# The feed-forward input of a streaming encoder step: eight block products against seven

## What is computed

```python
    x = x + gt1 * (merged @ w_out)
    h2 = rmsnorm(x, g_norm[1]) * (1 + sc2) + sh2
    u, gg = jnp.split(h2 @ w_ffn_in, 2, axis=-1)
    x = x + gt2 * ((jax.nn.silu(gg) * u) @ w_ffn_out)
```

## Time and profile before

| | |
|---|---|
| median of 3 runs | 1094.04 us (1091.89 to 1094.91) |
| profiled execution | span 1095.1 us, and no time around the span is listed |
| TensorE busy | 1045.0 us, 95% of the span |
| VectorE, ScalarE, GpSimd busy | 395.5, 366.5, 368.7 us |
| mean granted clock of TensorE | 0.980 |
| loads of the feed-forward input | 44 of 512 KB, 4.6 us from issue to landing |
| wait at the start of the feed-forward output | 0.3 us of TensorE, for GpSimd's `w_lo` |

### The profile page before, as it was taken

One profiled execution on the slowest core, in us unless ns is written; L12 is line 12 of the kernel. 1 busy time (PEld: TensorE's weight loads), 2 busy tenths in 40 slices (PEclk: granted clock), 3 DMA queues, 4 the chain that ended last, 5 costly groups with the idle time before them and its releaser, 6 DMA issues.

```text
span 1095.1 us, 25416 instructions
## 1 busy us (share of the span) xinstructions
PE 1045.0 (95%) x10988; PEld 966.9 (88%) x10988; DVE 395.5 (36%) x926; ACT 366.5 (33%) x745; POOL 368.7 (34%) x252
## 2 busy tenths in 40 slices
PE   6999999999998988989898999999999999999997
PEld 3899989999996766777787999999999999999997
DVE  4400000194045676566556576222222222200003
ACT  4443333353444444345232233322322232211112
POOL 2165433343316061401160333333343334344331
PEclk8899999999999999899998999999999999999999
DMA  9986666343311000020341532233222322132322
GB/s 358 352 276 235 234 206 198 99 139 119 113 42 36 18 7 22 13 82 3 131 130 43 198 116 58 77 92 99 77 77 83 107 78 65 55 104 79 92 67 82
DMA packets 118174, 122.23 MB, mean 112 GB/s; under 512 B 5396, under 2 KB 102848, under 8 KB 115656
## 3 DMA queue, kind: packets, MB, share of 16 engines
q1 hardware_dynamic: 112864, 111.86, 31.8%
q10 hardware_dynamic: 5224, 9.10, 2.5%
HBM read 108.33 MB, written 15.23 MB: 113 GB/s over the span
## 4 chain that ended last, share of the span: by engine, by line
PE 86%; DVE 7%; issue 3%; ACT 3%; POOL 1%; ACTq 1%; DVEq 0%; POOLq 0%
PE ps L1566 83%; PE ps L1917 2%; DVE s_sb L1306 1%; PE ps L1817 1%; POOL w_lo L595 1%; DVE s_sb L1340 1%; ACT x_sq L743 0%; DVE xn L1118 0%; DVE gring L1477 0%; DVE Pb L1277 0%; DVE y_sb L1549 0%; DVE mt L1479 0%; ACT mgh L1031 0%; DVE XX L1287 0%; ACTq L729 0%
## 5 line engine op out<-in xcount | busy, mean ns | idle before, releaser
L595 POOL TENSOR_TENSOR w_lo<-w_raw,w_hi 128x2048 fp32r<-128x2048 f32 (+1 forms) x66 | 282.3, 4277 | 564.0 <-ACT w_hi L753 544.9
L1566 PE MATMUL ps<-hh,w_hi 128*128 128x274 f32 x1376 | 290.0, 293 | 2.7 <-DVE hl L1128 2.0
L1566 PE MATMUL ps<-hh,w_lo 128*128 128x274 f32 x1376 | 288.1, 292 | 0.0
L1566 PE MATMUL ps<-hl,w_hi 128*128 128x274 f32 x1376 | 286.6, 291 | 0.0
L1566 PEld LDWEIGHTS ps<-hh,w_hi 128*128 128x128 f32 x1376 | 219.0, 190 | 12.8 <-issue 11.2
L1566 PEld LDWEIGHTS ps<-hh,w_lo 128*128 128x128 f32 x1376 | 218.7, 190 | 0.8 <-issue 0.8
L1566 PEld LDWEIGHTS ps<-hl,w_hi 128*128 128x128 f32 x1376 | 219.0, 190 | 0.0
L753 ACT ACTIVATE w_hi<-w_raw 128x2048 fp32r<-128x2048 f32 (+1 forms) x66 | 117.5, 1781 | 106.6 <-PE ps L1566 101.1
L1566 PE MATMUL ps<-ah,w_hi 128*128 128x274 f32 x352 | 75.3, 290 | 0.3 <-POOL w_lo L595 0.3
L1566 PE MATMUL ps<-ah,w_lo 128*128 128x274 f32 x352 | 75.4, 290 | 0.0
L1566 PE MATMUL ps<-al,w_hi 128*128 128x274 f32 x352 | 75.2, 290 | 0.0
(11 more groups left out here) (375 smaller groups left out, 1537.8 us busy)
## 6 DMA issues: line engine op xcount, KB each, us to landing
w_raw<-in_w_ffn_in SPq DMA_DIRECT2D x44, 512.0 KB, 4.6
w_raw<-in_w_in SPq DMA_DIRECT2D x42, 512.0 KB, 5.0
ada_l<-in_w_ada SPq DMA_DIRECT2D x16, 1024.0 KB, 6.4
ada_w<-in_w_ada SPq DMA_DIRECT2D x8, 1024.0 KB, 13.6
w_raw<-in_w_ffn_out SPq DMA_DIRECT2D x16, 384.0 KB, 4.0
w_raw<-in_w_ffn_out SPq DMA_DIRECT2D x16, 320.0 KB, 3.4
g_d<-gst SPq DMA_DIRECT2D x16, 274.0 KB, 2.4
gring<-g_d SPq DMA_DIRECT2D x16, 274.0 KB, 3.2
```

The source lines that it names most:

```text
L595: pool.tensor_tensor(w_lo[:, s, 0:cols], w_raw[:, s, 0:cols], w_hi[:, s, 0:cols].bitcast(F32), ALU.subtract).then_inc(lo_done, 1)
L1566: return pe.matmul(out, lhsT, rhs, start=start, stop=stop)
```

## The change

From the second unit on, the feed-forward input is a product of 2 x 2 blocks in Winograd's form of Strassen's method. The blocks of the weight: gate and up columns, even and odd inner blocks. The blocks of the tokens: the two halves of 274, even and odd inner blocks. Seven products of 4 inner blocks each take the place of eight. The new parts:

- `token_sums`: four sums of token blocks for each pair of inner blocks, on VectorE into `tq`, in the output projection, behind every second tile. `token_high` rounds them on ScalarE (1096 columns), `token_low` subtracts on GpSimd.
- `raw_sums` and `second_sums`: four sums of weight blocks (512 columns) for each unit, on VectorE, written into PSUM banks 4 to 7.
- `block_high` rounds the seven weight blocks of 512 columns on ScalarE. `block_low` on VectorE takes the low part of the four summed ones, `blocks_low` on GpSimd that of the three plain ones. `ws_hi` and `ws_lo` have one slot for each product, so a block of the next unit is made once its product of this unit is done.
- `seven` on TensorE: the products 0, 2, 4 and 6 go on adding in one bank, 3 and 5 in another. Four times ScalarE copies an intermediate state into `rest` (`kept`), and the next product into that bank waits for it.
- `gate_first`, `up_second`, `up_first`, `gate_second` on VectorE put the quarters of the result together and multiply by the norm factor.
- The activated values are kept unsplit in `a_f`; their 22 high and low parts are made during the last unit and as the output product begins (`act_high`, `act_low`), the high parts in the place of the tokens' `hh`, `hl`, `th` and `tl`. VectorE also makes the low part of the first two output units.
- Semaphores are used again under new names, and the output tiles `y_sb` lie elsewhere. Loads are of the same size; the first waits differ.

The core of the diff (SP's loads, addresses and the first, plain unit are left out):

```diff
+        U_ST, NST = U_UP + 1, NUP - 1
+        NPR, NPL, NSM = 7, 3, 4
+        PRODUCT_BANK = (0, 2, 0, 3, 0, 3, 0)
+        SUM_BANK = {2: 4, 3: 5, 4: 6, 6: 7}
+        PLAIN, SUMMED = (0, 1, 5), (2, 3, 4, 6)
...
+            def token_low(c):
+
+                pool.wait_ge(th_done, TH + c + 1)
+                pool.tensor_tensor(tl[:, :, c, :], tq[:, c % 2, :, :], th[:, :, c, :].bitcast(F32), ALU.subtract)\
+                    .then_inc(tl_done, 1)
+            for i in range(U_WO, U_UP + 1):
+                low(i, i % 2)
+                if i >= U_WO + 2:
+                    token_low(i - U_WO - 2)
+            token_low(HK - 1)
+
+            def blocks_low(i, s):
+
+                for p in PLAIN:
+                    pool.wait_ge(wshi_done, i * NPR + (WSHI + p + 1 - U_ST * NPR))
+                    pool.tensor_tensor(slot_of(ws_lo, p), block_source(s, p), slot_of(ws_hi, p).bitcast(F32), ALU.subtract)                        .then_inc(wslo_done, 1)
+            two_by_two(pool, U_ST, NST, blocks_low)
...
+            def token_high(c):
+
+                act.wait_ge(tq_done, TQ + 4 * c + 4)
+                act.activation(th[:, :, c, :], tq[:, c % 2, :, :], ACT.Copy).then_inc(th_done, 1)
+
+            def block_high(i, s, p):
+
+                if p in PLAIN:
+                    act.wait_ge(raw_in[s], i * 16 + (32 - 16 * s))
+                else:
+                    act.wait_ge(wsum_done, i * NSM + (WSUM + {2: 4, 3: 3, 4: 2, 6: 4}[p] - U_ST * NSM))
+                if isinstance(i, int) and i == U_ST:
+                    act.wait_ge(unit_mm, U_UP + (p >= 4))
+                else:
+                    act.wait_ge(prod_mm, i * NPR + (PROD + p + 1 - (U_ST + 1) * NPR))
+                act.activation(slot_of(ws_hi, p), block_source(s, p), ACT.Copy).then_inc(wshi_done, 1)
...
+            def kept(i, s, which):
+
+                p = (0, 2, 3, 4)[which]
+                act.wait_ge(prod_mm, i * NPR + (PROD + p + 1 - U_ST * NPR))
+                if which < 2:
+                    act.wait_ge(quad_ev, i * 4 + (QUAD + (5, 7)[which] - U_ST * 4))
+                act.activation(rest[:, which, :], product_out(s, p), ACT.Copy).then_inc(rest_ev, 1)
...
+            def up(i, s):
+                kept(i, s, 0)
+                block_high(i + 1, 1 - s, 0)
+                block_high(i + 1, 1 - s, 1)
+                kept(i, s, 1)
+                block_high(i + 1, 1 - s, 2)
+                kept(i, s, 2)
+                block_high(i + 1, 1 - s, 3)
+                kept(i, s, 3)
+                for p in range(4, NPR):
+                    block_high(i + 1, 1 - s, p)
+                gated_silu(i)
...
+            def act_high(c):
+
+                act.wait_ge(prod_mm, PROD + LAST + (1 if c < KD else 5 if c < 12 else 3 if c < 14 else 7))
+                act.wait_ge(act_f32, c + 1)
+                act.activation(act_hi(c), a_f[:, c, :], ACT.Copy).then_inc(ah_done, 1)
...
+            def token_sums(c):
+
+                if c >= 2:
+                    dve.wait_ge(tl_done, TL + c - 1)
+                b11, b12, b21, b22 = [tmp_a[:, r, h * H:(h + 1) * H] for r in range(2) for h in range(2)]
+                t1, t2, t4, t3 = [tq[:, c % 2, b, :] for b in range(4)]
+                tt(t1, b12, b11, ALU.subtract).then_inc(tq_done, 1)
+                tt(t3, b12, b22, ALU.subtract).then_inc(tq_done, 1)
+                dve.wait_ge(tq_done, TQ + 4 * c + 1)
+                tt(t2, b22, t1, ALU.subtract).then_inc(tq_done, 1)
+                dve.wait_ge(tq_done, TQ + 4 * c + 3)
+                tt(t4, b21, t2, ALU.subtract).then_inc(tq_done, 1)
...
+            def raw_sums(i, s):
+
+                dve.wait_ge(raw_in[s], i * 16 + (32 - 16 * s))
+                if not (isinstance(i, int) and i == U_ST):
+                    dve.wait_ge(dlo_done, i * NSM + (DLO - U_ST * NSM))
+                a11, a21, a22 = raw_block(s, 0, 0), raw_block(s, 1, 0), raw_block(s, 1, 1)
+                tt(block_source(s, 3), a21, a11, ALU.subtract).then_inc(wsum_done, 1)
+                tt(block_source(s, 4), a21, a22, ALU.add).then_inc(wsum_done, 1)
+
+            def second_sums(i, s):
+
+                s2, s3 = block_source(s, 2), block_source(s, 3)
+                dve.wait_ge(wsum_done, i * NSM + (WSUM + 1 - U_ST * NSM))
+                tt(s2, s3, raw_block(s, 1, 1), ALU.add).then_inc(wsum_done, 1)
+                dve.wait_ge(wsum_done, i * NSM + (WSUM + 3 - U_ST * NSM))
+                tt(block_source(s, 6), raw_block(s, 0, 1), s2, ALU.subtract).then_inc(wsum_done, 1)
+
+            def block_low(i, s, p):
+
+                dve.wait_ge(wshi_done, i * NPR + (WSHI + p + 1 - U_ST * NPR))
+                tt(slot_of(ws_lo, p), block_source(s, p), slot_of(ws_hi, p).bitcast(F32), ALU.subtract).then_inc(dlo_done, 1)
...
+            def quarter(i, s, out, p, of, kept_):
+                dve.wait_ge(rest_ev, i * 4 + (REST + 1 + kept_ - U_ST * 4))
+                dve.wait_ge(prod_mm, i * NPR + (PROD + p + 1 - U_ST * NPR))
+                return tt(out, of, rest[:, kept_, :], ALU.add).then_inc(quad_ev, 1)
+
+            def gate_first(i, s):
+
+                dve.wait_ge(act_f32, i - U_UP)
+                quarter(i, s, ff_g[:, 0:H], 1, product_out(s, 1), 0)
+                dve.wait_ge(quad_ev, i * 4 + (QUAD + 9 - U_ST * 4))
+                tt(ff_g[:, 0:H], ff_g[:, 0:H], rstd2[:, 0:H], ALU.mult)
+
+            def up_second(i, s):
+                quarter(i, s, ff_a[:, H:W], 4, rest[:, 2, :], 3)
+
+            def up_first(i, s):
+
+                quarter(i, s, ff_a[:, 0:H], 5, product_out(s, 5), 1)
+                dve.wait_ge(quad_ev, i * 4 + (QUAD + 11 - U_ST * 4))
+                tt(ff_a[:, :], ff_a[:, :], rstd2[:, :], ALU.mult).then_inc(ffa_f32, 1)
+
+            def gate_second(i, s):
+                dve.wait_ge(prod_mm, i * NPR + (PROD + NPR - U_ST * NPR))
+                tt(ff_g[:, H:W], product_out(s, 6), rstd2[:, H:W], ALU.mult).then_inc(quad_ev, 1)
+
+            def finish_unit(i):
+                dve.wait_ge(ffa_f32, i + (FFA + 1 - U_ST))
+                activated(i)
+
+            def gate_up(i, s, sums=True):
+                gate_first(i, s)
+                second_sums(i + 1, 1 - s)
+                block_low(i + 1, 1 - s, 2)
+                block_low(i + 1, 1 - s, 3)
+                up_second(i, s)
+                block_low(i + 1, 1 - s, 4)
+                up_first(i, s)
+                gate_second(i, s)
+                block_low(i + 1, 1 - s, 6)
+                if sums:
+                    raw_sums(i + 2, s)
+                finish_unit(i)
...
+            i, s = U_DN - 1, (U_DN - 1) % 2
+            gate_first(i, s)
+            for c in range(3):
+                act_low(c)
+            first_down_low(U_DN, U_DN % 2)
+            up_second(i, s)
+            act_low(3)
+            up_first(i, s)
+            gate_second(i, s)
+            for c in range(4, 6):
+                act_low(c)
+            finish_unit(i)
+            first_down_low(U_DN + 1, (U_DN + 1) % 2)
+            for c in range(6, FT):
+                act_low(c)
...
+                for p, x in enumerate((b11, b21, t2, t3, t1, t4, b22)):
+                    if p in PLAIN:
+                        pe.wait_ge(wslo_done, i * NPL + (WSLO + PLAIN.index(p) + 1 - U_ST * NPL))
+                    else:
+                        pe.wait_ge(dlo_done, i * NSM + (DLO + SUMMED.index(p) + 1 - U_ST * NSM))
+                    fresh = p in (0, 1, 3)
+                    if fresh:
+                        pe.wait_ge(quad_ev, i * 4 + (QUAD + {0: 4, 1: 5, 3: 7}[p] - U_ST * 4))
+                    else:
+                        pe.wait_ge(rest_ev, i * 4 + (REST + {2: 1, 4: 2, 5: 3, 6: 4}[p] - U_ST * 4))
+                    xh, xl = x
+                    for c in range(HK):
+                        w = slice(p * QB + c * P, p * QB + (c + 1) * P)
+                        for j, (wt, xt) in enumerate(((ws_hi, xh), (ws_hi, xl), (ws_lo, xh))):
+                            ins = pe.matmul(product_out(s, p), wt[:, w], xt[c], start=fresh and c == 0 and j == 0,
+                                            stop=c == HK - 1 and j == 2, skip_group_check=not fresh)
+                    ins.then_inc(prod_mm, 1)
...
+            pe.wait_ge(dlo_done, DLO + NSM * NST)
+            for part_ in range(2):
+                pe.wait_ge(lo_done, U_DN - NST + part_ + 1)
+                for c, term in enumerate(down_terms(part_)):
+                    pe.wait_ge(act_done, part_ * KDN + c + 1)
+                    ins = product(T_DN, 2, part_, [term], part_ == 0 and c == 0, part_ == 1 and c == KDN - 1)
+                ins.then_inc(unit_mm, 1)
+            down_tile(1, 3)
```

223 lines of the change are left out of this document (159 added, 64 removed).

## The result

The changed kernel takes 1098.34 us, the median of 9 runs (1096.0 to 1101.9). The kernel before, run beside it, takes 1094.70 us (9 runs, 1090.9 to 1097.1). The ratio is 1.0035, with a 95% interval of 1.002 to 1.005. It is slower by some 3.8 us, where 15 were forecast. The time lies in the range, and the direction is right, but the size is not.

The account below looks back on a forecast made before the run. TensorE bounds the kernel; VectorE's round with holds was to set the new unit. Terms 8.7 + 1.7 + 1.4 + 2.4 - 1.5 + 2.5 = +15.2 on 1095.1 give 1110.3, less 1.1: 1109 us, range 1072 to 1127.

Parts of the forecast that it names:

- The bound before, and TensorE's gain: Feed-forward input: only TensorE counts; 84 matmuls in place of 96 cut a unit from 12.28 to 10.75 us.
- VectorE's own need: Feed-forward unit: VectorE alone, sixteen instructions and waits, needs 10.2 us (9.6 to 10.6), PSUM writes taken as free.
- the late sum 2: Feed-forward unit: VectorE's low part of sum 2 waits for ScalarE's rounding, behind the last weight sum: 0.60 plus 0.14 us.
- The holds: Feed-forward unit: GpSimd holds VectorE at the shared port 1.75 to 3.0 us; unit 12.4 us, +2.4 over 20 units.
- The layout: Unit timed from the last weight sum: GpSimd holds the scaling of 548, gated product's small part and gate's scaling.
- The output projection: Before the first feed-forward unit: token sums of 4.8 us and three holds of 2.4 make TensorE wait, +8.7 us.
- Clock and entering: Lower clock after the projection's wait, +1.7 us; product 0 waiting for the first unit's gate evacuation, +1.4 us.
- Leaving: Output product's start: 16 splits behind the last product make TensorE wait 1.9 us, second tile's weights 0.9 late; +2.5 us.
- rival 2: Feed-forward unit: one hold instead of two or three, unit 11.3 us, 1087 us in all; chance 0.18.
- The point from which the side changes: Feed-forward unit length that divides a faster from a slower kernel: 11.6 us.
- Rival 1: VectorE keeps up, holds fall into slack, unit 10.75 us: 1076 us, or 1067 without projection holds; chance 0.24.
- Rival 3: TensorE's idle 1.5 to 2.4 us in every unit lowers its clock: 1139 us at the most; chance 0.08.

Follow-up runs that it names:

- experiment 1: Changed kernel with VectorE's second weight sums (sums 2 and 6) issued right behind the raw sums, ahead of the gated product: 1072.35 us, ratio 0.980.
- experiment 3: Changed kernel with GpSimd's low parts made in only 8 of each 128 columns from the second Strassen unit on: 1074.49 us, ratio 0.981.
- experiment 4: Changed kernel with GpSimd's low parts made in only 64 of each 128 columns from the second Strassen unit on: 1076.66 us, ratio 0.984.
- Experiment 2: Changed kernel with ScalarE's copy of product 3 put ahead of its rounding of sum 2: 1101.49 us, ratio 1.0049.
- experiment 5: Changed kernel with GpSimd's token low parts (groups 0 to 2) begun one step later, at VectorE's next residual: 1092.87 us, ratio 0.9976.
- number 7: Changed kernel with second weight sums early and GpSimd's token low parts in halves, each starting as VectorE starts a residual: 1065.80 us, ratio 0.9749; again 1067.49, 0.9739.
- number 6: Changed kernel with second weight sums early and GpSimd's token low parts begun one step later: 1069.63 us, ratio 0.9765.

## Why the prediction was right or wrong
**The bound before, and TensorE's gain: right.** A unit without waits takes 10.67 to 10.69 us in experiments 1 and 3, against 10.75 worked out and 12.28 before.

**VectorE's own need: right.** I had 10.2 us (9.6 to 10.6); experiment 4, and the changed kernel's unit less its holds, give 10.3 to 10.4. The write to PSUM is free as taken: a sum of 512 columns into PSUM takes 0.69 or 0.70, as from the earlier trace rows. Also as laid out are the late sum 2 (0.74 us of waiting), and ScalarE's order, which carries it on to product 5.

**The holds: the term that was mis-sized.** This is the step that failed. I took 12.4 - 10.2 = 2.2 us of holds in a unit, bounds 1.75 to 3.0. It had 1.4, and the unit took 11.77 us in place of 12.4, below my bounds of 11.9 to 13.2: 20 x 0.63 = 12.6 us in the sum. The layout had GpSimd take block 5 at 3.55, 0.15 us ahead of VectorE's scaling of 548, which was then to wait 1.0. In the trace VectorE's comes 0.05 us ahead, and GpSimd waits. The other two holds are the ones of the layout: the small part behind the large one (1.03 against 1.05), then the gate's scaling, which was over-sized as well (0.32 to 0.45 against 0.75). I had laid out the unit with a resolution of 0.1 us out of durations that I had rounded myself, and this meeting was decided by less. Experiment 2 shows nearly the same code at another outcome: 2.5 us of holds and a unit of up to 12.19. The Trainium skill states it in "SBUF — State Buffer", "Who interferes with whom": "Issue order, not op shape, decides who blocks." The meeting at 775.01 and 775.06 agrees. I used the page's rule of who collides and passed over this one.

**The output projection: mechanism right, size nearly.** +6.6 against +8.7. There were three holds as forecast, of 2.1 us in place of 2.4, and the sums, 1.5 a group in place of 1.6. Experiments 5 and 7 take the holds away in two steps (2.1, 1.0, 0), and TensorE's wait goes 5.27, 1.36, 0. For the sums alone I had +1.5. Number 7 still has the sums and needs 41.14 us from the second residual (632.63) to the first feed-forward unit (673.77), against 40.95 before: three groups of 1.5 us cost 0.2 when nothing of theirs is held.

**Clock and entering: too small.** I had +1.7 and +1.4. The clock behind the projection's wait cost what I took: 24 matmuls from 684.92 on last 4.97 us, where they lasted 3.26, 1.7 more. Product 0 then waited 0.4. What I did not have is the first two Strassen units. Product 5 waits 2.83 us in the first, 2.0 more than later, and behind it 14 matmuls run at 0.228 us in place of 0.128, from 712.78 to 715.98, 1.4 more. In the second it waits 1.61, 0.8 more. The last round takes 12.19, 0.4 more. My reading, which no experiment tests by itself, is that the first unit had no round behind it that would have given VectorE a start, so that the full lateness fell on one product. In all, entering and clock cost 1.7 + 0.4 + 2.0 + 1.4 + 0.8 + 0.4 = 6.7 us against the 3.1 forecast. So 3.6 of the 12.6 were taken back, and 9.0 is what the third row of the table is off. The two errors have opposite signs, and that is luck; without the second one the changed kernel would be about level with the one before.

**Leaving: right, smaller.** +1.1 against +2.5: waits of 1.3 at split 6 and 0.2 for the second tile's weights, for which I had 1.9 and 0.9.

**The rivals.** The changed kernel lies between the forecast (12.4) and rival 2 (one hold, 11.3). The point from which the side changes, a unit of 11.6, held: the unit came 0.17 us above it, and the result 0.35% above no change. In part that is luck, since the other terms' errors nearly cancel (projection and leaving 3.5 us too large, entering and clock 3.6 too small). Rival 1 was priced well: its 1076 us with a unit at TensorE's own time, and 1067 with no holds in the projection either, stand beside 1072 to 1077 (experiments 1, 3 and 4) and 1066 (number 7). Rival 3 (the clock falls in each unit) is refuted for the gaps that came: with 0.8 us in each unit the clock was 1.00, and in experiment 2 with 1.1 to 1.24 us as well. Its own gaps of 1.5 to 2.4 us in every unit never came.

What stays open: when the clock falls behind a single wait (the last section has gaps of like length with and without it). And ScalarE's rounding of sum 2 waits for both late sums (`{2: 4, ...}` in `block_high`), and starts at 783.35 behind the one of 782.54, though the sum that it reads was written by the instruction of 781.82. No run lets it start behind that one alone, which might fill most of the 0.74 us without moving the sums.

## What to carry to other kernels
Add up the round of the engine that a change loads: own work, the waits that nothing fills, and the holds. Compare the sum with the bound's own time. Here 10.4 + 1.4 stood against 10.67, and taking away either the 1.4 of holds or the 1.5 that went with the late sums gave the whole 1.1 us back. Where two engines share a port, don't forecast one number for the holds. Which engine waited here was settled by 0.05 us, so forecast both outcomes. Look at every place where the two can meet: when one hold went (experiment 5), the work behind it moved, and two raw sums that had been free were held for 1.6 us. Better still, order the work so that GpSimd runs beside instructions that read PSUM, as in number 7.

## What the runs showed that I had not expected
- GpSimd is held too: its low part of 512 columns takes 1.28 us alone and 1.84 when VectorE's scaling of 548 columns was issued 0.05 us ahead of it.
- That a VectorE scaling by a per-partition number with one SBUF input is held was in the forecast, but not why. It takes 0.49 us for 512 columns, against 0.69 for a pair of inputs, and 2.60 at 648.21 beside GpSimd's 2.33. The Trainium skill names this in "SBUF — State Buffer", "Who interferes with whom", for instructions in a 2-port mode. The shorter duration fits that, but no run shows the mode itself.
- The length of one wait does not say by itself whether the clock falls. After 2.83 us at 711.35 the first ten matmuls still ran 0.128 us apart, the next 14 at 0.228, then 0.128 again. In number 6, 2.52 us were followed at once by 12 slow ones, and in experiment 4 a wait of 1.7 us (702.70) by 14. In experiment 5, waits of 2.53 and 2.86 us were followed by none, as was the 1.61 of the changed kernel's second unit. After 5.27 us the clock was 0.66 over 680 to 690.
